# Front end of a two-block transformer kernel: one chunk's convolution on VectorE, shifted copies issued from two queues, norms and spatial products inside dense blocks 12 to 15

## What is computed

```python
h = modulate(rmsnorm(x, norm1_g[i]), shift1, scale1)
z = h @ w_in[i] + b_in[i]
u, v, val, gate = jnp.split(z, [D_A, 2 * D_A, 2 * D_A + D_B], axis=-1)
y_a = spatial_gating_mixer(gelu(u), gelu(v), a_ln_g[i], a_ln_b[i], a_spatial_w[i], a_spatial_b[i])
y_b = conformer_conv_mixer(val, gate, b_conv_w[i], b_conv_b[i], b_gn_g[i], b_gn_b[i])
y = jnp.concatenate([rmsnorm(y_a, out_norm_a_g[i]), rmsnorm(y_b, out_norm_b_g[i])], axis=-1)
x = x + gate1[:, None, :] * (y @ w_out[i])
...
# spatial_gating_mixer, chunks of 128 positions, 8 heads
v = layernorm(v, ln_g, ln_b)
mixed = jnp.einsum('hts,bcshd->bcthd', causal_w, v) + b_s
return u * mixed
...
# conformer_conv_mixer, width 31, 512 channels, 8 groups of 64
y = val * jax.nn.sigmoid(gate)
y = causal_depthwise_conv(y, conv_w) + conv_b
y = layernorm_per_group(y, gn_g, gn_b)
return jax.nn.silu(y)
```

## Time and profile before

| | us |
|---|---|
| three timed runs, median | 1881.59 (1880.83 to 1882.97) |
| profiled execution, its own time | 1883.0 |
| profiled execution, span | 1881.3 |
| TensorE matmul busy | 1725.2 (92%) |
| VectorE busy | 879.6 (47%) |
| ScalarE busy | 634.3 (34%) |
| GpSimd busy | 191.4 (10%) |

### The profile page before, as it was taken

How to read it: one execution, slowest core, us unless ns; L and a number is a source line. 1 busy time by engine, 2 the same in 40 slices (tenths; PEclk the granted TensorE clock), 3 DMA queues, 4 the chain that set the end, 5 groups by cost and what they waited for, 6 DMA issues and landing times.

```text
span 1881.3 us, 22086 instructions
## 1 busy us (share of the span) xinstructions
PE 1725.2 (92%) x8159; PEld 1343.0 (71%) x8159; DVE 879.6 (47%) x1307; ACT 634.3 (34%) x929; POOL 191.4 (10%) x187
## 2 busy tenths in 40 slices
PE   2799698999999949999999899999999799999996
PEld 1467476888888837766666688888887588888884
DVE  6533566443332344165556644444434844444323
ACT  1223333223222223355555344443223533333221
POOL 4010206950000042000000000000200000000000
PEclk9899798999999969999999799999998799999998
DMA  7675033532322204111111132233221032223221
GB/s 284 202 209 180 23 134 122 178 132 92 105 92 95 84 28 114 56 35 46 34 34 46 45 101 92 97 100 110 94 86 57 23 100 90 100 97 114 92 77 45
DMA packets 49976, 180.83 MB, mean 96 GB/s; under 512 B 6336, under 2 KB 7008, under 8 KB 49792
## 3 DMA queue, kind: packets, MB, share of 16 engines
q1 hardware_dynamic: 46912, 169.51, 27.0%
q0 software_dynamic: 3008, 10.59, 2.1%
HBM read 173.55 MB, written 2.10 MB: 93 GB/s over the span
## 4 chain that ended last, share of the span: by engine, by line
PE 67%; issue 21%; DVE 6%; ACT 2%; POOL 1%; DMA 1%; SPq 1%; POOLq 0%; DVEq 0%; ACTq 0%
PE bank L316 15%; PE bank L317 15%; PE bank L318 15%; PE bank L1107 3%; PE bank L1108 2%; PE bank L1109 2%; PE bank L1167 2%; PE bank L1211 2%; PE bank L962 2%; PE bank L1187 1%; DVE ada_acc L1549 1%; POOL tmp L461 1%; PE bank L386 1%; PE bank L1092 1%; PE bank L1265 1%
## 5 line engine op out<-in xcount | busy, mean ns | idle before, releaser
L264 DVE TENSOR_TENSOR w_lo<-raw,w_hi 128x1024 fp32r<-128x1024 f32 (+1 forms) x236 | 318.7, 1350 | 742.7 <-ACT w_hi L260 742.7
L316 PE MATMUL bank<-h_hi,w_hi 128*128 128x512 f32 x1248 | 495.1, 397 | 5.9 <-DVE h_lo L480 3.6
L317 PE MATMUL bank<-h_lo,w_hi 128*128 128x512 f32 x1248 | 488.5, 391 | 0.0
L318 PE MATMUL bank<-h_hi,w_lo 128*128 128x512 f32 x1248 | 488.2, 391 | 0.0
L260 ACT ACTIVATE w_hi<-raw 128x1024 fp32r<-128x1024 f32 (+1 forms) x236 | 265.4, 1125 | 638.9 <-PE bank L318 577.2
L316 PEld LDWEIGHTS bank<-h_hi,w_hi 128*128 128x128 f32 x1248 | 235.8, 189 | 66.8 <-issue 9.7
L318 PEld LDWEIGHTS bank<-h_hi,w_lo 128*128 128x128 f32 x1248 | 236.0, 189 | 49.7
L317 PEld LDWEIGHTS bank<-h_lo,w_hi 128*128 128x128 f32 x1248 | 236.4, 189 | 48.2 <-issue 1.0
L316 PE MATMUL bank<-hid_hi,w_hi 128*128 128x512 f32 x528 | 210.6, 399 | 0.0
L317 PE MATMUL bank<-hid_lo,w_hi 128*128 128x512 f32 x528 | 210.4, 398 | 0.0
L318 PE MATMUL bank<-hid_hi,w_lo 128*128 128x512 f32 x528 | 210.2, 398 | 0.0
(11 more groups left out here) (302 smaller groups left out, 1927.6 us busy)
## 6 DMA issues: line engine op xcount, KB each, us to landing
raw<-in_f2i SPq DMA_DIRECT2D x88, 512.0 KB, 3.2
raw<-in_ffi SPq DMA_DIRECT2D x44, 512.0 KB, 3.3
raw<-in_f2o SPq DMA_DIRECT2D x32, 704.0 KB, 4.0
ada_w<-in_ada_w SPq DMA_DIRECT2D x32, 512.0 KB, 4.4
raw<-in_att_w SPq DMA_DIRECT2D x24, 512.0 KB, 3.2
raw<-in_ffo SPq DMA_DIRECT2D x16, 704.0 KB, 4.0
raw<-in_ada_w SPq DMA_DIRECT2D x16, 512.0 KB, 4.8
raw<-in_w_in SPq DMA_DIRECT2D x16, 512.0 KB, 6.4
```

Of the source, the lines that this page charges most:

```text
L264: nc.vector.tensor_tensor(WL[par][:, 0:kc * P], RAW[s][:, 0:kc * P], WH[par][:, 0:kc * P].bitcast(F32), ALU.subtract).then_inc(wlo, 1)
L316: pe_.matmul(bank[:, :], w_h, hi[:, k0 + k, :], start=start and k == 0, stop=False)
L317: pe_.matmul(bank[:, :], w_h, lo[:, k0 + k, :], start=False, stop=False)
L318: last = pe_.matmul(bank[:, :], w_l, hi[:, k0 + k, :], start=False, stop=stop and k == kc - 1)
```

## The change

- Chunk 0's convolution leaves TensorE. VectorE computes it by 31 taps and one addition (`tap`), in two accumulators in turn, in its iterations 2 to 7, six or five at a time. The tap weights are 31 further columns of the vector `vec`.
- Chunks 1 to 3 still go through shifted copies. SyncE issues those for shifts 0 and 1, ScalarE those for shifts 2 and 3, eight each, ahead of its work for blocks 4, 6 and 8. Convolutions stand after blocks 5, 7 and 9.
- Group means and variances go in the order 1, 0, 2, 3.
- The ada steps are spread anew: one with each of blocks 2 to 7, two with w_out blocks 0 to 3; their column sums stand after blocks 7, 13 and w_out block 6 (they were after 5, 9 and 13). The small loads (`LNR`, `WS`, `BS`) move from n = 3 to n = 9, `BS` in two copies instead of eight.
- Transposes and turn go inside block 12, scales after 12 and 13, spatial products inside block 14, sum and broadcast of norm b inside block 15, those of norm a inside the first two w_out blocks. There the second block's part is now issued ahead of the first's.
- The upper and lower splits of w_out's second block move behind block 15.

```diff
+TAP_STEPS = {n: 6 if n < 4 else 5 for n in range(2, 8)}
+ADA_STEPS = [2, 2, 1, 1, 1, 1, 1, 1, 2, 2, 2, 2, 2, 0, 0, 0] + [2, 2, 2, 2, 1, 1, 1, 1]
+CHUNKS = (1, 0, 2, 3)
...
-                if c >= 2:
-                    sp.wait_ge(j1["conv"], c - 1)
-                for t in range(4):
+                if c == 3:
+                    sp.wait_ge(j1["conv"], 1)
+                for t in range(2):
                     for g in range(4):
-                        sp.dma_start(YP[32 * t:32 * t + 32, c % 2, g, :],
-                                     Y[32 * g:32 * g + 32, c, t:t + S + 4 * (QUADS - 1)]).then_inc(j1[f"yp{c % 2}"], 16)
+                        sp.dma_start(YP[32 * t:32 * t + 32, (c - 1) % 2, g, :],
+                                     Y[32 * g:32 * g + 32, c, t:t + S + 4 * (QUADS - 1)]).then_inc(j1[f"yp{(c - 1) % 2}"], 16)
...
+            def ada_loads(end):
+                while loaded[0] < end:
+                    i = loaded[0]
+                    sp.wait_ge(ada_used, i - 3)
+                    load_ada(i, ada_w[ADA_A + i])
+                    loaded[0] += 1
             for n in range(12):
                 sp.wait_ge(wlo, n + 1)
                 load(n % 4, w_in[n + 4], D)
-                if n in (2, 4, 6, 8):
+                if n in (4, 6, 8):
                     shifted(n // 2 - 1)
-                for i in (2 * n + 4, 2 * n + 5):
-                    sp.wait_ge(ada_used, i - 3)
-                    load_ada(i, ada_w[ADA_A + i])
-                if n == 3:
+                if n:
+                    ada_loads(sum(ADA_STEPS[:n]) + 4)
...
                 for step in range(C + LAG):
+                    if step >= LAG:
+                        if step == LAG:
+                            pe_.wait_ge(ev[1], bank_count)
+                            pe_.wait_ge(wlo, n + 2)
+                        m = part(1, order[step - LAG], step - LAG)
+                    if at is not None:
+                        at(step)
                     if step < C:
                         if step == 0:
                             pe_.wait_ge(ev[0], bank_count)
                             pe_.wait_ge(wlo, n + 1)
                         pe_.wait_ge(n_lo, ready + step + 1)
-                        m = part(0, order[step], step)
+                        m0 = part(0, order[step], step)
                         if step == C - 1:
-                            m.then_inc(mm, 1)
-                    if step >= LAG:
-                        if step == LAG:
-                            pe_.wait_ge(ev[1], bank_count)
-                            pe_.wait_ge(wlo, n + 2)
-                        m = part(1, order[step - LAG], step - LAG)
+                            m0.then_inc(mm, 1)
...
-                    pe_.wait_ge(j1["gx"], c - 1)
+                    pe_.wait_ge(j1["gx"], 2)
...
+            def inside(n, k):
+                if n == 12 and k == 4:
+                    v_tokens()
+                if n == 12 and k == 6:
+                    group_turn()
+                if n == 14 and k in (2, 6):
+                    spatial(k // 4 * 2)
+                    spatial(k // 4 * 2 + 1)
+                if n == 15 and k == 0:
+                    pe_sum(nj["nb"])
+                if n == 15 and k == 6:
+                    pe_.wait_ge(j1["gx"], CA)
+                    pe_bcast(nj["nb"], PS[4])
             first_two(0, 1, range(C), nj["n1"].lo)
             for n in range(2, 16):
                 pe_.wait_ge(ev[n % 2], n // 2 + 1)
-                block(n, n % 2, C, HH, HL, 0, PS[n % 2], True, True)
-                if n in (3, 5, 7, 9):
+                block(n, n % 2, C, HH, HL, 0, PS[n % 2], True, True, None, lambda k: inside(n, k))
+                if n in (5, 7, 9):
                     conv((n - 3) // 2)
-                if n in (4, 6, 8, 10):
-                    group_mean((n - 4) // 2)
-                if n in (5, 7, 9, 11):
-                    group_var((n - 5) // 2)
-                if n in (5, 9, 13):
-                    j = n // 4 + 1
+                for e in {6: (0,), 8: (1, 2), 10: (3,)}.get(n, ()):
+                    group_mean(e)
+                for e in {7: (0,), 9: (1, 2), 11: (3,)}.get(n, ()):
+                    group_var(e)
+                if n in (7, 13):
+                    j = 2 + n // 13
                     ada_sums(j, PS[5], ada_used, C * (j - 1))
-                if n == 12:
-                    group_turn()
-                    v_tokens()
-                if n in (13, 14):
-                    group_scale(2 * (n - 13))
-                    group_scale(2 * (n - 13) + 1)
-                if n == 14:
-                    spatial(0)
-                    spatial(1)
-            spatial(2)
-            spatial(3)
-            pe_sum(nj["nb"])
-            pe_.wait_ge(j1["gx"], CA)
-            pe_bcast(nj["nb"], PS[4])
-            pe_sum(nj["na"])
-            pe_bcast(nj["na"])
-            first_two(N0["w_out"], O0["w_out"] // 2, (4, 5, 6, 7, 0, 1, 2, 3), nj["nb"].lo)
+                if n in (12, 13):
+                    group_scale(2 * (n - 12))
+                    group_scale(2 * (n - 12) + 1)
+            def other_half(step):
+                if step == 3:
+                    pe_sum(nj["na"])
+                if step == 4:
+                    pe_bcast(nj["na"])
+            first_two(N0["w_out"], O0["w_out"] // 2, (4, 5, 6, 7, 0, 1, 2, 3), nj["nb"].lo, other_half)
             for n in range(2, C):
                 pe_.wait_ge(ev[n % 2], O0["w_out"] // 2 + n // 2)
                 block(N0["w_out"] + n, n % 2, C, HH, HL, 0, PS[n % 2], True, True)
+                if n == 6:
+                    ada_sums(4, PS[5], ada_used, C * 3)
...
+            def shifted(c):
+                act.wait_ge(j1["y"], c + 1)
+                if c == 3:
+                    act.wait_ge(j1["conv"], 1)
+                for t in range(2, 4):
+                    for g in range(4):
+                        act.dma_start(YP[32 * t:32 * t + 32, (c - 1) % 2, g, :],
+                                      Y[32 * g:32 * g + 32, c, t:t + S + 4 * (QUADS - 1)]).then_inc(j1[f"yp{(c - 1) % 2}"], 16)
+            def before_block(n):
+                if n in (4, 6, 8):
+                    shifted(n // 2 - 1)
+                if n in (6, 8, 10):
+                    c = (n - 4) // 2
+                    act.wait_ge(j1["conv"], c)
+                    act.activation(CV[:, c, :], PS[2 + (c - 1) % 2][:, :], ACT.Identity, bias=vcol("conv_b", c)).then_inc(j1["cv"], 1)
+                for e in {7: (0,), 9: (1, 2), 11: (3,)}.get(n, ()):
+                    act.wait_ge(j1["xc"], e + 1)
+                    if e >= 2:
+                        act.wait_ge(j1["var"], e - 1)
+                    act.activation(TMP[:, e % 2, :], CV[:, CHUNKS[e], :], ACT.Square).then_inc(j1["sq"], 1)
+                if n == 12:
+                    act.wait_ge(j1["v32"], 1)
+                    act.activation(R32[:, 1, :], R32[:, 0, :], ACT.Sqrt).then_inc(j1["sd"], 1)
+                    for i in range(TC):
+                        act.wait_ge(j1["vt"], i + 1)
+                        act.activation(VT[:, i, :], (PS[2], PS[3], PS[4], PS[7])[i][:, :], ACT.Copy).then_inc(j1["vtc"], 1)
+                    act.wait_ge(j1["r8t"], 1)
+                    act.activation(R8[:, :], NS[0:GB, :], ACT.Copy).then_inc(j1["r8"], 1)
+                if n == 14:
+                    for c in range(CA):
+                        group_silu(c)
+                    act_squares(nj["nb"], CA, lambda k: CV[:, k, :], lambda k: act.wait_ge(j1["yb"], k + 1), lambda k: Y[:, k, 0:S])
+                if n == 15:
+                    act_squares(nj["na"], 3, lambda k: YA[:, k, :], lambda k: act.wait_ge(j1["ya"], k + 1), sq_p1)
...
+            def last_square(k):
+                if k == 1:
+                    act.wait_ge(j1["ya"], CA)
+                    act.activation(sq_p1(3), YA[:, 3, :], ACT.Square).then_inc(n_sq, 1)
+                    split_hi(17, 1, 1, C, ROUND["w_out"])
+            act_parts(nj["nb"], CA, k0=CA, behind=last_square)
...
+            def tap(k):
+                w = VEC[:, COL["conv_1"] + k:COL["conv_1"] + k + 1]
+                dst = CV[:, 0, :] if k % 2 == 0 else ACC
+                if k >= 2:
+                    dve.wait_ge(j1["tap"], k - (1 if k < TAPS else 0))
+                if k == 0:
+                    ins = dve.tensor_scalar(dst, Y[:, 0, 0:S], w, vcol("conv_b", 0), ALU.mult, ALU.add)
+                elif k == 1:
+                    ins = dve.tensor_scalar(dst, Y[:, 0, 1:1 + S], w, None, ALU.mult)
+                elif k < TAPS:
+                    ins = dve.scalar_tensor_tensor(dst, Y[:, 0, k:k + S], w, dst, ALU.mult, ALU.add)
+                else:
+                    ins = dve.tensor_tensor(CV[:, 0, :], CV[:, 0, :], ACC, ALU.add)
+                ins.then_inc(j1["tap"], 1)
...
+                    tokens_normed()
+                if n == 13:
+                    tokens_scaled()
+                    group_mult(0)
```

(28 more changed lines are left out.)

192 lines of the change are left out of this document (88 added, 104 removed).

## The result

The changed kernel takes **1853.7 us** (median of four runs, 1849.68 to 1854.03) where the kernel before takes 1882.28 beside it (four runs, 1880.83 to 1883.87): a ratio of 0.9843, 95% interval 0.9832 to 0.9855. The forecast was 1852 in 1844 to 1864. The profiled execution took 1853.88 us for a span of 1852.1; the sum said 1853.4.

The account below looks back on a forecast made before the run. TensorE's waits in the front end, 50 to 287 us, were taken as the bound, the first for issuing copies. Terms -20.9, -12.8 and +4.1 sum to -29.6: 1853.4 profiled, 1852 timed, range 1844 to 1864.

Parts of the forecast that it names:

- the first hole: TensorE busy 15.7 of 24.7 us from 76.1 to 100.8; claimed issuing sixteen copies, 11.12 us, is the wait.
- Block 2's split: Front end: the split comes a part later, since block 0's last part is issued later; cost 0.3 us.
- A: End of block 3 to start of block 12, 96.6 us: claimed to become 75.7, gain 20.9 us.
- S: Taps on VectorE, iterations 2 to 7: 1.75 to 2.40 us each beside GpSimd, up to 1901; chance 0.03.
- 9.5 us to the end of the broadcast: First two w_out blocks: norm b's four chunks at VectorE's pace, then norm a's sum, power, diagonal and broadcast, 9.5 us.
- 1.5 for a new start: First two w_out blocks, beside the eight parts left (6.8): 1.5 us charged for restarting at the 1.2 GHz level.
- B: Start of block 12 to end of first two w_out blocks, 74.7 us: claimed to become 61.9, gain 12.8.
- Stage C: The w_out blocks: loss 4.1 us, from an evacuation wait (0.8), two ada steps per iteration (1.5), an ada sum (1.8).
- nothing moves: From 290 us on the code is the same: claimed no change there, 0 us.
- D: Rival: no lower clock in block 14 and first w_out blocks, VectorE's w_out excess hidden: 1846; chance 0.13.
- Q: Rival: SyncE and ScalarE queues share one rate, eight issues take 11 us on each: +9, 1861; chance 0.11.
- T: Rival: the rearranged tail gives nothing, its waits return in a stream that starts and stops: 1865; chance 0.13.

Follow-up runs that it names:

- after_again: The changed kernel, unchanged, run again in a later session beside the two small edits combined: 1852.09 us, ratio 0.9836.
- after: The changed kernel itself, measured against the kernel before: 1853.7 us, ratio 0.9843.
- ada_even: Changed kernel with four ada steps moved from w_out blocks 0 to 3 into block 14: 1852.35 us, ratio 0.9842.
- early_sum: Changed kernel with norm a's sum at step 2 instead of 3 of the first two w_out blocks, its mean and broadcast earlier: 1850.91 us.

## Why the prediction was right, and where its terms were not

**The bound of the first hole: right.** It was issue time. With one queue 6.8 us come back, with two the wait is gone.

**Copies on ScalarE: right, and a little better.** Taken 0.70 us an issue, measured 0.68 (5.46/8), landing 2.4 at the median. The gated chunk came at 80.3 to 81.0, as forecast (80.6). The wait of 1.2 us before the convolution did not come in this execution; in after_again it was 0.9. The group mean waited 0.33 us for ScalarE's evacuation behind its issues, forecast 0.1: cover used up, as the text said.

**Block 2's split, 0.3 us: too small.** The wait there is 0.53 and block 2 starts at 66.41, 1.5 us later than before (0.4 to 1.9 over all traces). With the missing wait of 1.2 it cancels but for 0.5: A was 20.4 and not 20.9.

**Taps at 0.67: right**, 0.66 a step where they stand in a row. Rival S's price does occur, once. VectorE, and GpSimd building weight tiles:

```profile
95.08 0.74 DVE L1644 SCALAR_TENSOR_TENSOR tmp<-y_pad,vec_sb,tmp 128x512 f32<-128x512 f32 x1
95.74 2.41 DVE L1644 SCALAR_TENSOR_TENSOR conv<-y_pad,vec_sb,conv 128x512 f32<-128x512 f32 x1
98.07 0.74 DVE L1644 SCALAR_TENSOR_TENSOR tmp<-y_pad,vec_sb,tmp 128x512 f32<-128x512 f32 x1
```

```profile
95.58 2.02 POOL L828 TENSOR_TENSOR conv_w_tiles<-vec_sb,eye 128x1024 f32<-128x1024 f32 x1 [56.01 <-PE bank L979]
```

GpSimd's operation ends at 97.60, the tap at 98.15: it runs as if it had started when GpSimd's was done. The Trainium skill says so of the two engines ("SBUF — State Buffer", section "SBUF: two separate sides": a VectorE operation with two inputs in SBUF and a GpSimd operation that reads SBUF exclude each other for a whole instruction); by this row it agrees. GpSimd has just this one operation while the taps run, so one of 32 is hit, and S was rightly 0.03. What was wrong in S is its slope: "0.87 us a tap are free, each 0.1 above costs 3.2". The free 28 us are about right (waits of 3.8 where 31.0 us of operations were to fit), but past that point the price starts steeply, 8 to 10 us for 3 us of excess, with stretches at the lower clock behind the waits, and then hardly rises: 10.9 us for 12.3 us of excess. A forecast near such an edge needs the step and not the slope.

**Scales: right in place, smaller.** The new wait before the second pair is 0.84 us, forecast 1.4, and the pair then takes 2.85 us instead of 1.98 at the lower level. Block 14 started 20.85 us after block 12 (20.2 forecast, 0.65 late) and block 15 at 32.9 (32.1). Block 14 took 12.1 us, where 9.9 and 2 for its cold start were charged: those 2 us were there.

**Norm b under block 15: right.** Sum at 185.92, broadcast at 190.95, no wait at either; put back behind it, 3.5 us are lost. The wait of the first w_out matmul is 2.27 (2.3 forecast).

**The step that failed: "9.5 us to the end of the broadcast".** It measured 13.3 (11.5 in the second trace of the kernel after). 3.3 of the 3.8 us are the clock at its lower level, for which the prediction charged nothing in this term: in ada_even's trace, with the clock up and the same order on VectorE, it is 10.0. What the other 0.5 is stays open. VectorE's order, which puts a last lower part ahead of norm a's mean, was meant to be in the 9.5; with the sum and the mean moved up it is 7.9. The first low part of norm a then waits 2.23, as forecast (2.3). The clock was charged once, later, as "1.5 for a new start", and did not cost it there: the parts left took 7.1 us for 6.8 and 1.5. With 0.8 us of lateness at the end of block 15 that makes B's 3.4: 0.8 and 3.8, less 1.2.

**Stage C: right.** +3.7 for +4.1: the wait for the evacuation is 1.11 (1.2 forecast), iterations come every 5.89 us (5.95), and evening the steps out gives back 1.2 of the 1.5.

**Behind 290 us: "nothing moves" failed by 3.1 us**, and this is why the total looks better than its terms: it makes up for stage B. That the sum came out within 0.4 us is luck.

Rivals. D (1846): the clock is low in block 14 and at 200 us in after, so not. The one execution at 1846.21 is early_sum's, with another order and the clock up at 200 us. Q (shared rate): out, 5.46 and 5.12 us side by side. T (the tail gives nothing): out, 9.4 us. S: out, with the slope mended.
